# Shared room for weights asked for ahead, norms by tile, and a column norm between attention steps, in a two-block kernel

## The reference, cut to what matters

```python
def first_block(x, ...):
    shift1, scale1, gate1, shift2, scale2, gate2 = split(silu(c) @ w_ada + b_ada, 6)
    h = rms_norm(x, norm1_g) * (1 + scale1) + shift1
    q, k, v, b_gate, c_gate, u = split(h @ w_in + b_in)       # widths 512 128 128 512 512 512
    attn = head_rms_norm(window_attention(q, k, v, sinks))    # 8 heads of 64, window 128
    conv = head_rms_norm(b_gate * conv3(c_gate * u))
    x = x + gate1 * (concat(attn, conv) @ w_out + b_out)
    h2 = rms_norm(x, norm2_g) * (1 + scale2) + shift2
    x = x + gate2 * peer_layer(h2)       # 8 heads, top 16 of 16384 experts: gelu(h2 . u_e) * v_e
    return rms_norm(x, final_g)

def second_block(x, ...):
    hy_in, q, k, v, pool_in = split(rms_norm(x, norm1_g_2) @ w_in_2)     # 768 512 512 512 256
    y_hy = long_convolution(short_conv(hy_in))                # 256, by cosine and sine tables
    y_na = neighbourhood_attention(q, k, v, rpb)              # 512, 8 heads
    y_pool = pool_mixer(pool_in)                              # 256, windows 2 4 8 16
    x = x + concat(rms_norm(y_hy), rms_norm(y_na), rms_norm(y_pool)) @ w_out_2
    x = x + expert_choice_moe(rms_norm(x, norm2_g_2))         # 16 experts, 64 tokens each, ff 2048
    return rms_norm(x, final_g_2)
```

## Time and profile before

| | us |
|---|---|
| median of 3 runs | 3017.55 (3015.62 to 3020.02) |
| profiled execution, own time | 3017.46 |
| its span, first to last instruction | 3015.6 |
| PE busy | 2603.6 (86%) |
| DVE busy | 1419.1 (47%) |
| ACT busy | 842.5 (28%) |
| POOL busy | 690.5 (23%) |

### The profile page before, as it was taken

The page is one execution under the profiler, slowest core; times in us unless marked ns, Lnnn a source line. Parts: engine busy times, 40 slices in busy tenths (PEclk is TensorE's granted clock), DMA queues, the critical chain, the costliest instruction groups (busy, mean ns, idle before and its releaser), DMA issues. The chain is left out here.

```text
span 3015.6 us, 33514 instructions
## 1 busy us (share of the span) xinstructions
PE 2603.6 (86%) x12653; PEld 1829.1 (61%) x12653; DVE 1419.1 (47%) x2354; ACT 842.5 (28%) x1393; POOL 690.5 (23%) x433
## 2 busy tenths in 40 slices
PE   5988888999999979999998689677978888788786
PEld 2755678999999978888886566452322232223222
DVE  4357419997787747888787425541100000010001
ACT  2235213335767643333332223410000000000001
POOL 0042006677888842222221020000000000000000
PEclk8989899999999989999999799788999999999999
DMA  5444305558999999999995231139999999999996
GB/s 222 132 160 164 112 15 171 172 174 273 355 347 370 375 340 357 351 355 353 351 359 207 91 118 69 52 156 420 421 420 422 421 421 421 421 421 421 421 421 277
DMA packets 245685, 869.42 MB, mean 288 GB/s; under 512 B 28608, under 2 KB 97728, under 8 KB 192953
## 3 DMA queue, kind: packets, MB, share of 16 engines
q1 hardware_dynamic: 188960, 703.12, 60.9%
q0 software_dynamic: 38016, 138.43, 12.0%
q10 hardware_dynamic: 18584, 26.23, 2.4%
HBM read 812.10 MB, written 55.60 MB: 288 GB/s over the span
## 5 line engine op out<-in xcount | busy, mean ns | idle before, releaser
L702 PE MATMUL val_banks<-val_v,val_coef_split 128*128 128x512 f32 x2304 | 525.0, 390 | 17.5 <-DVE val_coef_split L87 17.5
L702 PEld LDWEIGHTS val_banks<-val_v,val_coef_split 128*128 128x128 f32 x2304 | 434.4, 189 | 108.1 <-DVE val_v L87 17.8
L947 PE MATMUL moe_up_ps<-all_raw_first,all_h_rows 128*64 128x512 f32 x1696 | 416.4, 600 | 71.5 <-DMA all_raw_first<-in_w_up 52.2
L581 PE MATMUL dots_dot_ps<-one_acts,dots_u_split 128*128 128x384 f32 x2064 | 374.1, 337 | 18.1 <-POOL dots_u_split L87 18.0
L581 PEld LDWEIGHTS dots_dot_ps<-one_acts,dots_u_split 128*128 128x128 f32 x2064 | 358.5, 189 | 21.3 <-POOL dots_u_split L87 10.7
L947 PEld LDWEIGHTS moe_up_ps<-all_raw_first,all_h_rows 128*64 128x64 f32 x1696 | 137.8, 137 | 317.4 <-issue 316.3
L1066 DVE TENSOR_TENSOR all_x<-moe_y_ps,all_x 128x512 f32<-128x512 f32 x64 | 44.1, 691 | 560.6 <-PE moe_y_ps L913 560.5
L87 POOL TENSOR_TENSOR dots_u_split<-dots_u_raw,dots_u_split 128x1024 fp32r<-128x1024 f32 x86 | 227.0, 2640 | 254.0 <-ACT dots_u_split L82 252.9
L964 PE MATMUL moe_y_ps<-all_raw_first,moe_hid_t 128*64 128x512 f32 x848 | 203.9, 597 | 43.8 <-DMA all_raw_first<-in_w_down 24.3
L82 ACT CAST val_v<-pe_shared 128x2048 fp32r<-128x2048 f32 x64 | 122.6, 1916 | 353.9 <-PE val_banks L702 345.5
L1136 POOL DMA_INDIRECT val_v_rows<-in_peer_v,one_expert x128 | 124.2, 970 | 409.9 <-DVE val_banks L653 388.6
(11 more groups left out here) (385 smaller groups left out, 3388.1 us busy)
## 6 DMA issues: line engine op xcount, KB each, us to landing
all_raw_first<-in_w_gate SPq DMA_DIRECT2D x106, 1024.0 KB, 27.0
all_raw_first<-in_w_up SPq DMA_DIRECT2D x106, 1024.0 KB, 27.4
all_raw_first<-in_w_down SPq DMA_DIRECT2D x106, 1024.0 KB, 27.3
pe_shared<-in_peer_v SPq DMA_DIRECT2D x64, 1024.0 KB
dots_u_raw<-in_u_tiles SPq DMA_DIRECT2D x86, 512.0 KB
expert_dots<-dots_gelu ACTq DMA_DIRECT2D x128, 192.0 KB
expert_weights<-pe_shared SPq DMA_DIRECT2D x48, 512.0 KB
pe_shared<-expert_dots SPq DMA_DIRECT2D x64, 384.0 KB
```

Source lines behind the costliest of these rows:

```text
L581: last = self.nc.tensor.matmul(self.banks[:, q % 2, 0:DENSE], self.split[q % 3][:, u_part, k], self.h_t[:, h_part, k, T - DENSE:T], start= ...
L702: last = nc.tensor.matmul(banks[:, 2 * (t + 1) + half, :], coef_split[:, b, c_part, a, t * P:(t + 1) * P], v[:, b, v_part, a, half * BANK: ...
L947: last = nc.tensor.matmul(up_ps[of(e), b, :], xs_t(i)[:, k, of(e)], w[e][:, b * BANK:(b + 1) * BANK], start=(k == 0), stop=(k == KD - 1))
```

## The change

One buffer `shared` now spans both blocks, and `w_raw`, `ada`, `attn`, the mixers' rooms and the values' buffers are parts of it (`room`). A class `Ahead` asks for the first six pieces of a product's weights in the phase before: in the opening (behind the four w_ada pieces' use), in the first output phase (behind w_raw's use), in the end of the value phase, and in "an2". `product_phase` loads only the pieces from the seventh on; ScalarE waits once for all six. The wait for the spectrum's store moves from the opening's SP to VectorE's start in `first_mixer`.

In `peer_first_phase` the 48 sets go behind tiles 4 + 60 n / 48 instead of 4 + 4 n / 3, and the last span's parts are stored two to a tile.

In `peer_value_phase` TensorE does the last turn by tile of tokens, and both norms, the transposes and the splits into `acts` follow by tile in the same block; "nf" and "n3" go. The gain table is loaded in the second mixer's SP list, and `load_columns` there goes.

The column norm "hn" goes; its squares, products with ones, root, reciprocals, scalings and splits stand in the second mixer at steps 23 to 34 (`NORM_STEP` is 26).

```diff
+class Ahead:
+    PLACES, TILES = 6, 2
+    def __init__(self, sem, room, w_dram, first_cols):
+        self.sem, self.w, self.first_cols = sem, weight_tiles(w_dram), first_cols
+        self.raw = room[:, 0:self.PLACES * self.TILES * BANK].rearrange("p (b k n) -> p b k n", b=self.PLACES, k=self.TILES)
+    def ask(self, sp, p):
+        n, h = p // (KD // self.TILES), p % (KD // self.TILES)
+        sp.dma_start(self.raw[:, p], self.w[:, h * self.TILES:(h + 1) * self.TILES,
+                                            self.first_cols[n]:self.first_cols[n] + BANK]).then_inc(self.sem, 16)
+    def wait(self, eng):
+        eng.wait_ge(self.sem, 16 * self.PLACES)
...
-        raw = s.sb("raw", [P, RAW, TILES, width]) if raw is None else raw[:, 0:RAW * TILES * width // D, :].rearrange(
-            "p a n -> p (a n)").rearrange("p (b k n) -> p b k n", b=RAW, k=TILES)
+        raw = ahead.raw
...
-                    for to, src in chunks[n][0](raw[:, p % RAW], slice(h * TILES, (h + 1) * TILES)):
-                        sp.dma_start(to, src).then_inc(loaded[p % RAW], 16)
+                        for to, src in chunks[n][0](raw[:, p % RAW], slice(h * TILES, (h + 1) * TILES)):
+                            sp.dma_start(to, src).then_inc(loaded[p % RAW], 16)
...
-                    act.wait_ge(loaded[p % RAW], need[p])
+                    if p >= RAW:
+                        act.wait_ge(loaded[p % RAW], need[p])
+                    elif p == 0:
+                        ahead.wait(act)
...
+                sp.wait_ge(v_lo, n_turns - 1)
+                ahead.ask(sp, 0)
+                ahead.ask(sp, 1)
+                sp.wait_ge(v_lo, n_turns)
+                ahead.ask(sp, 2)
+                ahead.ask(sp, 3)
+                sp.wait_ge(coef_lo, n_turns)
+                ahead.ask(sp, 4)
+                ahead.ask(sp, 5)
...
+                act.wait_ge(eps_ready, 1)
+                n = 0
+                def squares(t, total, root, root_ready, ready):
+                    nonlocal n
+                    act.wait_ge(ready, t + 1)
+                    if n >= 2:
+                        act.wait_ge(squared, n - 1)
+                    nc.scalar.activation(square[:, n % 2, :], x[:, t, :], ACT.Square,
+                                         accum_out=total[:, t:t + 1]).then_inc(squared, 1)
+                    n += 1
+                    act.wait_ge(squared, n)
+                    nc.scalar.activation(root[:, t:t + 1], total[:, t:t + 1], ACT.Sqrt, scale=1.0 / D,
+                                         bias=eps[:]).then_inc(root_ready, 1)
+                def last_norm(t):
+                    squares(t, total1, root1, root1_ready, added)
+                def first_norm(t):
+                    squares(t, total2, root2, root2_ready, normed)
+                def high(t):
+                    for half in range(2):
+                        act.wait_ge(turned, 2 * t + half + 1)
+                        split_hi(nc.scalar, part_t(0, t, half), turned_bank(t, half)).then_inc(hi_ready, 1)
+                last_norm(0)
+                last_norm(1)
+                first_norm(0)
+                last_norm(2)
+                first_norm(1)
+                high(0)
+                last_norm(3)
+                first_norm(2)
+                high(1)
+                first_norm(3)
+                high(2)
+                high(3)
...
-                step = Steps(dve, dve_step)
                 dve.wait_ge(sparse.used, P)
-                for o in range(8):
-                    t, half = o // 2, o % 2
-                    cols = slice(half * BANK, (half + 1) * BANK)
-                    if o == 2:
-                        dve.wait_ge(summed, 2 + n_turns)
-                    step(nc.vector.tensor_tensor(part[:, o % 2, :], banks[:, o, :], gate[:, cols], ALU.mult))
-                    nc.vector.tensor_tensor(x[:, t, cols], part[:, o % 2, :], x[:, t, cols], ALU.add)
+                def add(t):
+                    if t >= 1:
+                        dve.wait_ge(tile_done, t)
+                    for half in range(2):
+                        cols = slice(half * BANK, (half + 1) * BANK)
+                        if t >= 1:
+                            dve.wait_ge(added, t)
+                        nc.vector.tensor_tensor(part[:, half, :], banks[:, 2 * t + half, :], gate[:, cols],
+                                                ALU.mult).then_inc(scaled, 1)
+                    for half in range(2):
+                        cols = slice(half * BANK, (half + 1) * BANK)
+                        dve.wait_ge(scaled, 2 * t + half + 1)
+                        ins = nc.vector.tensor_tensor(x[:, t, cols], part[:, half, :], x[:, t, cols], ALU.add)
+                    ins.then_inc(added, 1)
+                def last_norm(t):
+                    dve.wait_ge(root1_ready, t + 1)
+                    nc.vector.reciprocal(rstd1[:, t:t + 1], root1[:, t:t + 1]).then_inc(inv1_ready, 1)
+                    dve.wait_ge(inv1_ready, t + 1)
+                    nc.vector.scalar_tensor_tensor(out=x[:, t, :], in0=x[:, t, :], scalar=rstd1[:, t:t + 1], in1=last_g,
+                                                   op0=ALU.mult, op1=ALU.mult).then_inc(normed, 1)
+                def first_norm(t):
+                    dve.wait_ge(root2_ready, t + 1)
+                    nc.vector.reciprocal(rstd2[:, t:t + 1], root2[:, t:t + 1]).then_inc(inv2_ready, 1)
+                    dve.wait_ge(inv2_ready, t + 1)
+                    if t >= 2:
+                        dve.wait_ge(turned, 2 * (t - 1))
+                    nc.vector.scalar_tensor_tensor(out=h[:, t % 2, :], in0=x[:, t, :], scalar=rstd2[:, t:t + 1], in1=first_g,
+                                                   op0=ALU.mult, op1=ALU.mult).then_inc(h_ready, 1)
+                def low(t):
+                    for half in range(2):
+                        dve.wait_ge(hi_ready, 2 * t + half + 1)
+                        split_lo(nc.vector, part_t(1, t, half), turned_bank(t, half), part_t(0, t, half))
+                dve.wait_ge(g_loaded, 32)
+                add(0)
+                add(1)
+                last_norm(0)
+                add(2)
+                first_norm(0)
+                last_norm(1)
+                add(3)
+                low(0)
+                first_norm(1)
+                last_norm(2)
+                last_norm(3)
+                low(1)
+                first_norm(2)
+                first_norm(3)
+                low(2)
+                low(3)
...
+                pe.wait_ge(v_lo, n_turns)
+                pe.wait_ge(coef_lo, n_turns)
+                for t in range(DT):
+                    for a in range(2):
+                        for c_part, v_part in ((0, 0), (0, 1), (1, 0)):
+                            for half in range(2):
+                                last = nc.tensor.matmul(
+                                    banks[:, 2 * (t + 1) + half, :], coef_split[:, 1, c_part, a, t * P:(t + 1) * P],
+                                    v[:, 1, v_part, a, half * BANK:(half + 1) * BANK],
+                                    start=False, stop=(a == 1 and c_part == 1), skip_group_check=True)
+                    last.then_inc(tile_done, 1)
+                for t in range(NT):
+                    pe.wait_ge(h_ready, t + 1)
+                    for half in range(2):
+                        for j in range(4):
+                            c = 4 * half + j
+                            last = nc.tensor.transpose(turned_bank(t, half)[:, j, :], h[:, t % 2, c * P:(c + 1) * P], ident[:])
+                        last.then_inc(turned, 1)
...
-        after_tile = [LAG + 4 * n // 3 for n in range(SETS)]
+        after_tile = [LAG + (LEFT - 12) * n // SETS for n in range(SETS)]
+        LAST_SPAN = PARTS * (SPANS - 1)
+        def store_from(part):
+            staged_at = after_tile[PER_SPAN * (part // PARTS + 1) - 1]
+            return staged_at + 4 + part % PARTS if part < LAST_SPAN else staged_at + 4 + part % PARTS // 2
...
+                sp.wait_ge(used, PIECES)
+                for p in range(ahead.PLACES):
+                    ahead.ask(sp, p)
                 sp.wait_ge(spec_taken, NT)
                 sp.dma_start(spec_dram, spec).then_inc(spec_stored, 16)
-                sp.wait_ge(spec_stored, 16)
...
+                    if i == NORM_STEP:
+                        for g in range(2):
+                            taken(pe, G_BACK + g)
+                            for m in range(2):
+                                pe.wait_ge(norm_squared, 2 * g + m + 1)
+                                last = nc.tensor.matmul(side_ps[:, g, :], ones[:], norm_square[:, m, :] if g else short[:, m, :],
+                                                        start=(m == 0), stop=(m == 1))
+                            last.then_inc(side_done, 1)
...
+                    if i == 23:
+                        act.wait_ge(pool_y_ready, 2)
+                        act.wait_ge(out_ready, 4)
```

(58 more changed lines are left out.)

257 lines of the change are left out of this document (144 added, 113 removed).

## The result

| | before | changed |
|---|---|---|
| runs | 3015.62 to 3020.02 | 2970.47 to 2976.34 |
| median, us | 3017.23 | 2973.8 |
| profiled execution: span, own time | 3015.6, 3017.46 | 2968.6, 2970.47 |

The ratio is 0.9848, with a 95% interval of 0.9836 to 0.986: 43.4 us faster in the medians, where 47.3 were forecast. The forecast of 2970 is 3.8 us (0.13%) too low; the range held the time. One further execution of the changed kernel, in `again`, took 3350.07 us at a mean granted clock of 0.764 where the others had 0.956 to 0.959, and is left out of all medians and ratios.

The account below looks back on a forecast made before the run. The expert stage, a weight stream at the DMA engines' full 421 GB/s, was taken as bound and untouched, so savings ahead move the end. Six parts sum to -47.3 us from 3017.5: forecast 2970, range 2960 to 2982.

Parts of the forecast that it names:

- A: Opening to first projection: spectrum-store wait goes, first weights already on chip, clock stays up; -9.5 us.
- Rival 3: Opening: the early weight loads collide with the broadcast of the modulation rows; 2974 us, chance 0.05.
- B: First output projection to query product: the 5.16 us wait for first weights shrinks; -4.2 us.
- C: First expert-table phase: denser sets and earlier stores let the value phase start sooner, less late tiles; -7.0 us.
- rivals 2 and 4: Set stretch: denser sets gain nothing, 2977 us, chance 0.13; GpSimd bounds it, above 3018, 0.03 with similar mishaps.
- D: End of the weighing of v, both norms and first weights: second projection's product starts earlier; -19.6 us.
- E: Second mixer: column norm phase goes, saving 19.2 us, its work lengthens the steps; net -3.9 us.
- Rival 1: Second mixer: norm does not fit between steps, through table changes and clock drops; 2974 or 2976 us, chance 0.12.
- F: Attention norm and output product: added table load costs 1.0, wait for weights goes; -3.1 us.

Follow-up runs that it names:

- again: The changed kernel run once more without edits, as base for the other runs; median 2974.99 us of three, ratio 0.9853.
- warm2: Changed kernel plus unused extra TensorE products, one behind the opening's last and six ahead of the first product's first piece; one execution, 2975.4 us.
- fill_holes: Changed kernel plus 14 unused extra products in each of TensorE's two pauses in the second mixer's tail; one execution, 2970.48 us.
- norm_apart: Changed kernel with the column norm again a phase of its own behind the second mixer; median 2976.46 us, ratio 0.9859.

## Why the prediction was right, and where it was off

The direction, the bound (the expert stage starts earlier and keeps its length) and all six parts hold in sign and place. The sum of 47.3 is 3.9 us over the 43.4 of the medians, and the parts as measured add up to 43.3:

- **A, 7.3 for 9.5.** The border is right to 0.1. The step that failed is "with a pause of only 3.6 us I take the clock to stay at 2.4 GHz": it fell to 0.50, and the 2.1 counted for it were not there. `warm2` measures the term: 1.6. Rival 3 (loads against the broadcast) falls: the opening ends at 67.1 to 69.2 in the runs with the loads, 68.5 without.
- **B, 4.1 for 4.2,** by the rows 1.02 against 5.16.
- **C, 6.9 for 7.0,** the difference of two halves that were each 0.8 to 0.9 larger than forecast: 9.4 off the gap (8.6 forecast), some 2.5 given back by late tiles (1.6). That the set stretch stays TensorE's holds, so rivals 2 and 4 fall.
- **D, 20.7 for 19.6.** The tail is 28.2 for 29: VectorE is busy 26.0 us in it, where the sum had 27.0 of work, and idle for 2.2, where it had 2. From its end to the product it is 2.6 us for 2.8. How much of the 20.7 each piece gave (norms by tile, the block with the column table, weights asked for ahead) was not taken apart by a run.
- **E, 1.9 for 3.9.** The two pauses of 4 us came as forecast. What the steps gained in length is 17.3 and not 15.3, and the mis-sized term is the clock behind the pauses: 2.8 by `fill_holes`, within its bounds of 0 and 3 but charged with 1.5. The other 0.7 was not taken apart. Rival 1 is half right: its time, 2974, is what came, but by its clock and not by its table changes. In the rows above a load takes 1.28 and the next activation starts 0.01 behind it (1868.58 + 1.28 to 1869.87; the attention norm's, at 1896.20, is followed by its root at 1897.49). The drain that the Trainium skill ("ScalarE: Activation LUTs", "What ACT_TABLE_LOAD costs") puts there does not show.
- **F, 2.4 for 3.1.** The step that failed is "the wait of 5.06 less 0.99 goes": the loads land 12.4 us after the first is asked (1893.97 to 1906.40), not 11.4, and some 0.3 of the wait is left. The norm is 1.3 to 1.5 longer than before, where 1.0 was charged for its table load; by `norm_apart` it is as long without that load, since the gain rows land later with six loads behind them. That term had nearly the right size and the wrong cause.

Too much was forecast by 2.2 in A, 2.0 in E, 0.7 in F and 0.1 each in B and C, too little by 1.1 in D: 4.0 in all. That this is nearly the 3.9 is partly luck, since the stretches forecast at 0 gave some 1.5 more and the first mixer takes 3.3 back in some runs. The profiled execution, 2970.47, fell nearer to the forecast only because its opening and its first mixer were on the short side.

## What to carry over

A pause of TensorE costs more than its length: price each new one with the slower matmuls behind it, and look at the granted clock there before calling it short. Where a part of work is moved beside a loop without slack, the engine that holds is only the first price; taking it away gained 2.8 us here, and filling the pause that was left 4.8. When a transfer is moved ahead, look at the small one beside it on the same queue, on which the work may wait. When total times scatter by 3 us, cut the trace at the same rows in each run: the tail of the weighing was 30.83 or 30.84 us in eleven traces and the second mixer 174.8 to 175.5 in eight, where medians could not decide. This holds for some stretches only: the opening scattered by 2.1 us, the first mixer and the set stretch by over 3.
